# Scoring the sampled sequences' key pages four pairs at a time

## The chip, the cores and the metric

The kernel runs on one core of a Trainium2 chip. A core has TensorE (PE; its weight loads are listed as PEld), VectorE (DVE), ScalarE (ACT), GpSimd (POOL) and the queue engine SyncE (SP), and DMA engines that SP, ACT and POOL issue to. The metric is the device time of one execution in microseconds (us); the kernel before takes 1441.07 us in the median of three runs (1440.92 to 1441.21).

## The reference, cut to what matters

One inference step through two decoder layers: 256 prompt tokens and, in the same pass, 8 sampled sequences with 4 new tokens each. The second layer's mixer is sparse attention with three branches (compressed, selected blocks, window), 12 query heads on 3 key/value heads of width 64. For the selected-block branch each sampled sequence has 2048 past tokens in a paged cache: 16 pages of 128 tokens, whose numbers stand in `page_table`. The part that the change touches is the score of every sampled query against every past key of its own sequence:

```
k_b = cache_slc_kv[page_table[b]]            # sequence b: 16 pages x 128 tokens, 3 heads, 64 wide
s   = einsum('qhgd,nhd->qhgn', q_b, k_b)     # 4 tokens x 3 kv heads x 4 query heads x 2048 keys
s   = s * SCALE - slope * distance           # later: mask to the chosen blocks, softmax, values
```

## The kernel before, in words

The eight PSUM banks are handed back and forth by `banks`: `fill` (TensorE waits for a free bank), `filled`, `take` (a reader waits for a full bank), `give`, `wait_given`.

The stretch in question is a loop of TensorE over `n` = 0 to 13 (lines 879 to 892), about 895 to 1012 us into the span. It does two unrelated things side by side:

- Prompt attention in 12 units. In turn `n` TensorE scores unit `n+1` (`unit_scores`, L836 and L837), transposes the probabilities of unit `n-1` (`unit_turn`, L845) and multiplies unit `n-2` with its values (`unit_pv`, L860 and L862, and L856 in every second unit). Between these, VectorE adds the distance term and finds maxima (L1657 to L1662), ScalarE takes exponentials (L1246), VectorE normalises (L1669 to L1676), and ScalarE copies the transposes out.
- Key-page scores of the sampled sequences. Two sequences share the 128 partitions (an even one in the lower 64, an odd one in the upper 64), so there are four pairs `b`. A pair's stationary operand is 128 x 32 (`QBD[:, b, h, :]`). One scoring step (`page_scores`, L876) multiplies it with 512 keys, four pages, of head `h`: one matmul, 128 x 32 by 128 x 512, into 32 partitions of bank 7. ScalarE copies these to `S_SLC` (`scores_out`, recorded at the copy helper's line L1203) before the next step may fill bank 7. There are 4 pairs x 4 chunks of 4 pages x 3 heads = 48 steps, four in each turn from `n` = 2 to 13: after `unit_scores`, after `unit_turn`, and two after `unit_pv`.

The keys lie in the arena, in two halves of 16 pages' width each. Half `s` holds all 16 pages of one pair. SP loads the even sequences and POOL the odd ones (`load_key_pages`, L353 to L359), in rounds of four DMAs: a load of four page numbers into registers (L341), then for each page register work and one 96 KB DMA (L359). Pairs 0 and 1 are loaded before the loop starts; pair 2 is loaded once step 11 (the last of pair 0) has left its half, pair 3 after step 23. After step 35, SP loads the window keys into the lower half (`in_wink`, L1922) and after step 47 the window values into the upper half (`in_winv`, L1924).

After the loop TensorE turns the new values (L899), scores new tokens (L905, which waits for VectorE's copies of the queries, L1692, and these wait for the last `unit_pv`), compressed keys (L911) and window keys (L920, four pairs in the four column groups of the array). L920 releases the first value pages (L366), which SP and POOL load in the same kind of rounds into the arena, while the softmaxes run; the loads of the last sequences wait for the transposed probabilities (L973), and the last products with values (L952) wait for these pages.

Of the kernel before, what the change touches and what calls it, by code (L numbers as in the profile page):

```python
# [17 lines left out]
SP, POOL = mybir.EngineType.SP, mybir.EngineType.Pool  # L18

P = 128  # L20
# [3 lines left out]
B = 8  # L24
# [11 lines left out]
H = 3  # L36
G = 4
PAGE = 128
NPG = 16
PG_STEP = 4  # L40
# [3 lines left out]
WIN = 512  # L44
# [122 lines left out]
def trunk_kernel(nc, x_in, mem_in, cst1_in, cst2_in, slcd_in, prm_in, bmat_in, cmat_in, w8_in, wglu_in, wfi_in, wfo_in,  # L167
# [3 lines left out]
    with ctx:  # L171
# [12 lines left out]
        AR = sb("arena", 12288)  # L184
# [8 lines left out]
        PT = sb("pages", P, I32, 1)  # L193
# [83 lines left out]
        QBD = U[:, 8288:8672].rearrange("p (b h r) -> p b h r", b=4, h=H)  # L277
# [8 lines left out]
        S_SLC = U[:, 0:3 * 2080].rearrange("p (h n) -> p h n", h=H)  # L286
# [8 lines left out]
        KP = [AR[:, 6144 * s:6144 * s + 6144].rearrange("p (g h n) -> p g h n", g=NPG, h=H) for s in range(2)]  # L295
# [5 lines left out]
        BK = [ctx.enter_context(nc.psum_tensor(f"bank{b}", [P, 512], F32)) for b in range(8)]  # L301
        banks = Banks([sem(f"bank{b}_full") for b in range(8)], [sem(f"bank{b}_free") for b in range(8)])
# [22 lines left out]
        kpage_loaded = [[sem(f"key_pages{s}_{c}_loaded") for c in range(2)] for s in range(2)]  # L325
# [5 lines left out]
        qbd_done, q_done = sem("sample_query_blocks"), sem("sample_queries")  # L331
# [3 lines left out]
        ss_max, ss_exp, ss_prob = sem("sample_slc_max"), sem("sample_slc_exp"), sem("sample_slc_prob")  # L335

        def page_numbers(eng, which, b, i, pool_in):

            at = PT[0:1, bass.ds(i * PG_STEP + b * NPG, PG_STEP)]  # L340
            return nc.values_load_multi_w_load_instructions(at, engines=[which], min_val=0, max_val=pool_in.shape[0] - 1)[1]  # L341

        def page(pool_in, r):
            return pool_in[bass.ds(r, 1), :, :].rearrange("a p n -> p (a n)")

        def wait_memory_attention(eng, l, n):

            if n == 0:
                banks.take(eng, ("ms", l, 4))
            elif n == 1:  # L350
                banks.wait_given(eng, ("mo", l, 2))

        def load_key_pages(eng, which, b, s):  # L353

            with eng.Fori(0, NPG // PG_STEP) as i:
                for u, r in enumerate(page_numbers(eng, which, b, i, slck_in)):
                    lo = 64 * (b % 2)
                    dst = AR[lo:lo + 64, bass.ds(i * (384 * PG_STEP) + (6144 * s + 384 * u), 384)]
                    eng.dma_start(dst, page(slck_in, r)).then_inc(kpage_loaded[s][b % 2], 16)  # L359

        def load_value_pages(eng, which, b):
            s = VSLOT[b]
# [32 lines left out]
        n = 0  # L395
# [21 lines left out]
        def _(pe):  # L417
# [448 lines left out]

            def page_scores(step):

                b, c, h = step // 12, step // 3 % 4, step % 3
                if step % 12 == 0:  # L870
                    if b == 0:
                        pe.wait_ge(qbd_done, 1)
                    for parity in range(2):
                        pe.wait_ge(kpage_loaded[b % 2][parity], 256 * (b // 2 + 1))
                banks.fill(pe, ("sk", step), 7)
                ins = nc.tensor.matmul(BK[7][32 * b:32 * b + 32, :].rearrange("p (g n) -> p g n", n=P), QBD[:, b, h, :],  # L876
                                       KP[b % 2][:, 4 * c:4 * c + 4, h, :], start=True, stop=True)
# [160 lines left out]
        def _(act):  # L1038
# [193 lines left out]
                banks.give(C(PTC[0:NCP, 2 * n:2 * n + 2, :].rearrange("p g q -> p (g q)"), BK[5 + n % 2][0:NCP, :]), ("pct", n))  # L1232

            def scores_out(step):
                b, c, h = step // 12, step // 3 % 4, step % 3
                banks.take(act, ("sk", step))
                banks.give(C(S_SLC[32 * b:32 * b + 32, h, WIN * c:WIN * c + WIN], BK[7][32 * b:32 * b + 32, :]), ("sk", step))

            for n in range(14):
                if n < 12:  # L1240
                    act.wait_ge(u_max, n + 1)
                    for gg in range(2):
                        for t in range(2):
                            s = SU[n % 2][:, gg, P * t:P * t + P * (t + 1)]
                            j = 2 * t + gg
                            ins = A(s, s, ACT.Exp, bias=NM[n % 2][:, j:j + 1], accum_out=RS[n % 2][:, j:j + 1])  # L1246
                    ins.then_inc(u_exp, 1)
                if n >= 2:
                    scores_out(4 * (n - 2))
# [5 lines left out]
                if n >= 2:  # L1255
                    scores_out(4 * (n - 2) + 1)
# [4 lines left out]
                for j in range(2 if n >= 2 else 0):  # L1261
                    scores_out(4 * (n - 2) + 2 + j)
# [41 lines left out]
        def _(pool):  # L1304
# [71 lines left out]
            banks.take(pool, ("hc", 1, 1), B // 2 - 1)  # L1376
            query_blocks(1, 15)
            pool.wait_ge(memkv_stored, 32)
            for p in range(4):
                wait_memory_attention(pool, 1, p)  # L1380
                if p >= 2:
                    banks.take(pool, ("sk", 12 * p - 13))
                load_key_pages(pool, POOL, 2 * p + 1, p % 2)
# [6 lines left out]
        def _(dve):  # L1390
# [368 lines left out]
            banks.wait_given(dve, ("sk", 47))  # L1759
# [48 lines left out]
        def _(sp):  # L1808
# [106 lines left out]
            for p in range(4):  # L1915
                wait_memory_attention(sp, 1, p)
                if p >= 2:
# [5 lines left out]
            banks.take(sp, ("sk", 47))  # L1923
# [151 lines left out]
```

## Time and profile before

| | |
|---|---|
| timed runs | 1441.21, 1440.92, 1441.07 us |
| span of the profiled execution | 1438.6 us; the page gives no other time of it, so about 2.5 us of a run lie outside the span |
| PE busy | 1301.7 us (90% of the span) |
| DVE, ACT, POOL busy | 300.5, 247.6, 184.5 us |
| L876, key-page scores | 96 matmul instructions, 51.6 us busy, 11.5 us of PE idle time just before them |

Times in the rows below are microseconds from the start of the span. "Granted clock" is TensorE's clock as a share of full speed, 2.4 GHz; 0.50 means 1.2 GHz. A row of PE's timeline gives the start of a group of matmuls and the time to its modelled end; since matmuls overlap, the distance between the starts of two neighbouring rows is the better measure of what a piece costs.

### The profile page before, as it was taken

How to read it: one execution, taken by the hardware profiler on the slowest of the kernel's cores; microseconds unless marked ns; L12 is line 12 of the kernel's file. 1: busy time of each engine (PE TensorE's matmuls, PEld its weight loads, DVE VectorE, ACT ScalarE, POOL GpSimd, SP SyncE). 2: the span in 40 equal slices, each digit the busy share in tenths (PEclk: the TensorE clock that was granted, in tenths of full speed). 3: DMA queues.
4: the chain of work that ended last, by engine and by line, in shares of the span. 5: the costliest groups of instructions: out<-in, count | busy, mean ns of one | idle time of the engine just before them, and what ended most of it. 6: DMA issues, size and time to landing. Idle time of an engine off the chain costs nothing. (4 is left out here: it accounts for less than half of the span.)

```text
span 1438.6 us, 17417 instructions
## 1 busy us (share of the span) xinstructions
PE 1301.7 (90%) x6217; PEld 955.9 (66%) x6217; DVE 300.5 (21%) x670; ACT 247.6 (17%) x555; POOL 184.5 (13%) x254
## 2 busy tenths in 40 slices
PE   7969999999697999999989987898656889999996
PEld 6837666666675777777767866332445667777774
DVE  4112333432304000000040013432730130000002
ACT  3040011010112111100021112555310111010000
POOL 1002432534300000000000004031351000000000
PEclk9857999999598999999999956899877989999998
DMA  7605224330057343364333415043562314333332
GB/s 304 247 1 175 89 87 131 110 109 0 1 207 294 117 146 123 139 262 140 131 117 117 147 52 171 7 131 133 188 180 73 117 59 145 121 142 127 121 121 73
DMA packets 57937, 185.37 MB, mean 129 GB/s; under 512 B 8385, under 2 KB 39362, under 8 KB 47298
## 3 DMA queue, kind: packets, MB, share of 16 engines
q1 hardware_dynamic: 51314, 165.84, 34.0%
q0 software_dynamic: 6144, 12.59, 3.1%
q10 hardware_dynamic: 432, 6.29, 1.1%
q8 instruction: 32, 0.52, 0.2%
q14 instruction: 15, 0.12, 0.0%
HBM read 180.91 MB, written 10.02 MB: 133 GB/s over the span
## 5 line engine op out<-in xcount | busy, mean ns | idle before, releaser
L641 PE MATMUL bank<-normed,slabs 128*128 128x288 f32 x1408 | 347.2, 410 | 7.3 <-DVE normed L1406 7.3
L641 PEld LDWEIGHTS bank<-normed,slabs 128*128 128x128 f32 x1408 | 270.7, 192 | 83.8 <-issue 8.2
L670 PE MATMUL bank<-hidden,slabs 128*128 128x288 f32 x704 | 173.2, 406 | 1.9 <-DVE hidden L1444 1.9
L608 PE MATMUL bank<-arena,phase 128*128 128x384 f32 x512 | 170.7, 492 | 0.0
L670 PEld LDWEIGHTS bank<-hidden,slabs 128*128 128x128 f32 x704 | 133.6, 190 | 39.5 <-DVE hidden L1444 2.7
L608 PEld LDWEIGHTS bank<-arena,phase 128*128 128x128 f32 x512 | 96.9, 192 | 65.2 <-issue 1.5
L453 PE MATMUL bank<-normed,slabs 128*128 128x288 f32 x400 | 99.1, 411 | 3.7 <-DVE normed L1406 3.7
L453 PEld LDWEIGHTS bank<-normed,slabs 128*128 128x128 f32 x400 | 76.9, 193 | 25.5 <-issue 4.1
L1444 DVE TENSOR_TENSOR hidden<-projected,bank 128x288 f32 (+1 forms) x44 | 20.0, 454 | 322.6 <-PE bank L641 322.6
L581 PEld LDWEIGHTS bank<-projected,hidden 128*128 128x128 f32 x480 | 64.9, 220 | 6.3 <-DVE mixed L1536 2.9
L581 PE MATMUL bank<-projected,hidden 128*128 (+1 forms) x480 | 65.9, 302 | 2.7 <-DVE mixed L1536 2.7
L453 PE MATMUL bank<-mixed,slabs 128*128 128x288 f32 x256 | 66.5, 416 | 1.3 <-DVE mixed L1796 1.3
L1318 POOL COPY arena<-projected 64x32 f32<-64x32 f32 x8 | 1.6, 206 | 481.5 <-ACT projected L1064 481.2
L432 PE MATMUL bank<-normed,cst 128*128 128x288 f32 x128 | 45.9, 487 | 19.3 <-ACT normed L1044 11.5
L1399 DVE TENSOR_SCALAR rstd<-bank 128x288 f32<-128x288 f32 x8 | 3.7, 458 | 282.5 <-PE bank L432 282.5
L1110 ACT ACTIVATE normed<-bank 128x288 f32<-128x288 f32 x32 | 13.1, 410 | 285.1 <-PE bank L670 175.9
L876 PE MATMUL bank<-arena,phase 128*32 128x512 f32 x96 | 51.6, 620 | 11.5 <-ACT phase L1203 11.5
L453 PEld LDWEIGHTS bank<-mixed,slabs 128*128 128x128 f32 x256 | 49.9, 196 | 15.4 <-issue 1.4
L1119 ACT ACTIVATE projected<-bank 128x288 f32<-128x288 f32 x44 | 18.0, 410 | 202.1 <-PE bank L641 202.0
L359 POOL DMA_DIRECT2D arena<-in_slck x64 | 33.9, 530 | 124.2 <-issue 118.9
L432 PEld LDWEIGHTS bank<-normed,cst 128*128 128x128 f32 x128 | 28.7, 230 | 31.2 <-issue 20.2
L1338 POOL TENSOR_TENSOR phase_small<-normed,phase 128x512 f32<-128x512 f32 (+1 forms) x15 | 17.1, 1139 | 220.9 <-DVE normed L1555 220.9
(277 smaller groups left out, 1246.2 us busy)
## 6 DMA issues: line engine op xcount, KB each, us to landing
slabs<-in_wfi SPq DMA_DIRECT2D x44, 1024.0 KB, 4.7
slabs<-in_w SPq DMA_DIRECT2D x25, 1024.0 KB, 5.0
arena<-in_cmp SPq DMA_DIRECT2D x128, 192.0 KB, 2.7
slabs<-in_wfo SPq DMA_DIRECT2D x32, 704.0 KB, 4.0
arena<-in_slck SPq DMA_DIRECT2D x64, 96.0 KB, 2.9
arena<-in_slck POOLq DMA_DIRECT2D x64, 96.0 KB, 2.7
out_win_old<-in_winold SPq DMA_DIRECT2D x1, 6096.0 KB, 24.4
arena<-in_slcv POOLq DMA_DIRECT2D x48, 96.0 KB, 2.7
```

Of the source, the lines that this page charges most:

```text
L359: eng.dma_start(dst, page(slck_in, r)).then_inc(kpage_loaded[s][b % 2], 16)
L432: ins = nc.tensor.matmul(BK[7][:, 0:T], ones, Hn[:, m, :], start=(m == 0), stop=(m == 7))
L453: ins = nc.tensor.matmul(BK[b][:, 0:T], wt[:, k, c * P:c * P + P], rhs[:, k, :], start=(k == 0), stop=(k == kc - 1))
L581: ins = nc.tensor.matmul(BK[r][:, cc * width:cc * width + width], BT[r][:, c, :], tok(c // 4), start=True, stop=True)
L608: ins = nc.tensor.matmul(out.rearrange("p h (g s) -> p h g s", s=8), W1S[:, c, a, j, :], PG[u][:, :, c * 8 + j, :, :].rearrange("p g h s - ...
L641: ins = nc.tensor.matmul(BK[2 * (u % SLOTS) + c][:, 0:T], wt[:, k, c * P:c * P + P], Hn[:, k, :], start=(k == 0), stop=(k == KC - 1))
L670: ins = nc.tensor.matmul(BK[b][:, 0:T], wt[:, k, :], HD[:, 11 * kh + k, :], start=(kh + k == 0), stop=(kh * 11 + k == 21))
L876: ins = nc.tensor.matmul(BK[7][32 * b:32 * b + 32, :].rearrange("p (g n) -> p g n", n=P), QBD[:, b, h, :], KP[b % 2][:, 4 * c:4 * c + 4, h ...
L1110: A(Hn[:, m, :], BK[b][:, 0:T], ACT.Square).then_inc(sq_done, 1)
L1119: ins = A(Z[:, 8 + u % SLOTS, :], BK[2 * (u % SLOTS)][:, 0:T], ACT.Silu)
L1338: ch.tick(tt(hr, re, cos, ALU.mult))
L1444: banks.give(tt(dst, Z[:, 8 + u % SLOTS, :], BK[2 * (u % SLOTS) + 1][:, 0:T], ALU.mult), up)
```

## The change

The arena's halves no longer hold one pair each. Half `c % 2` now holds four pages, chunk `c`, of all eight sequences; so a scoring step `(c, h)` can be done for all four pairs at once. It issues four matmuls, one for each pair, to four different groups of 32 columns, which write the four quarters of bank 7, and ScalarE copies the whole bank, 128 x 512, in one operation. There are 12 steps instead of 48, one in each turn `n` from 2 to 13. The number of matmuls stays at 48, the DMAs and bytes stay the same, and the releases are renamed: chunk 2 is loaded after step 2, chunk 3 after step 5, the window keys after step 8, the window values after step 11.

```diff
-        KP = [AR[...].rearrange("p (g h n) -> p g h n", g=NPG, h=H) for s in range(2)]
+        KP = [AR[...].rearrange("p (b g h n) -> p b g h n", b=B // 2, g=PG_STEP, h=H) for s in range(2)]
...
-        def load_key_pages(eng, which, b, s):
-            with eng.Fori(0, NPG // PG_STEP) as i:
-                for u, r in enumerate(page_numbers(eng, which, b, i, slck_in)):
-                    lo = 64 * (b % 2)
-                    dst = AR[lo:lo + 64, bass.ds(i * (384 * PG_STEP) + (6144 * s + 384 * u), 384)]
-                    eng.dma_start(dst, page(slck_in, r)).then_inc(kpage_loaded[s][b % 2], 16)
+        def load_key_pages(eng, which, par, c):
+            s = c % 2
+            with eng.Fori(0, B // 2) as i:
+                at = PT[0:1, bass.ds(i * (2 * NPG) + (par * NPG + PG_STEP * c), PG_STEP)]
+                for u, r in enumerate(numbers_at(which, at, slck_in)):
+                    dst = AR[64 * par:64 * par + 64, bass.ds(i * (384 * PG_STEP) + (6144 * s + 384 * u), 384)]
+                    eng.dma_start(dst, page(slck_in, r)).then_inc(kpage_loaded[s][par], 16)
...
             def page_scores(step):
-                b, c, h = step // 12, step // 3 % 4, step % 3
-                if step % 12 == 0:
-                    if b == 0:
-                        pe.wait_ge(qbd_done, 1)
+                c, h = step // 3, step % 3
+                if step == 0:
+                    pe.wait_ge(qbd_done, 1)
+                if h == 0:
                     for parity in range(2):
-                        pe.wait_ge(kpage_loaded[b % 2][parity], 256 * (b // 2 + 1))
+                        pe.wait_ge(kpage_loaded[c % 2][parity], 256 * (c // 2 + 1))
                 banks.fill(pe, ("sk", step), 7)
-                ins = nc.tensor.matmul(BK[7][32 * b:32 * b + 32, :]..., QBD[:, b, h, :],
-                                       KP[b % 2][:, 4 * c:4 * c + 4, h, :], start=True, stop=True)
+                for b in range(B // 2):
+                    ins = nc.tensor.matmul(BK[7][32 * b:32 * b + 32, :]..., QBD[:, b, h, :],
+                                           KP[c % 2][:, b, :, h, :], start=True, stop=True)
                 banks.filled(ins, ("sk", step))
...
             for n in range(14):
-                more = iter(range(4 * (n - 2), 4 * (n - 1)) if n >= 2 else ())
                 if n < 11:
                     unit_scores(n + 1)
                 if n >= 2:
-                    page_scores(next(more))
+                    page_scores(n - 2)
                 if 1 <= n < 13:
                     unit_turn(n - 1)
                 if n >= 2:
-                    page_scores(next(more))
                     unit_pv(n - 2)
-                for step in more:
-                    page_scores(step)
...
-                banks.give(C(S_SLC[32 * b:32 * b + 32, h, WIN * c:WIN * c + WIN], BK[7][32 * b:32 * b + 32, :]), ("sk", step))
+                banks.give(C(S_SLC[:, h, WIN * c:WIN * c + WIN], BK[7][:, :]), ("sk", step))
...                                              # SP, and likewise POOL with parity 1
-            for p in range(4):
-                wait_memory_attention(sp, 1, p)
-                if p >= 2:
-                    banks.take(sp, ("sk", 12 * p - 13))
-                load_key_pages(sp, SP, 2 * p, p % 2)
-            banks.take(sp, ("sk", 35))
+            for c in range(NPG // PG_STEP):
+                wait_memory_attention(sp, 1, c)
+                if c >= 2:
+                    banks.take(sp, ("sk", 3 * c - 4))
+                load_key_pages(sp, SP, 0, c)
+            banks.take(sp, ("sk", 8))
```

On TensorE, one turn of the loop (here `n` = 3) before: the scoring steps are the rows of L876, `unit_turn` is L845, `unit_pv` is L860 and L862.

```order
L876 MATMUL bank<-arena,phase 32x512 [waits bank7_free]
L845 MATMUL bank<-cst,hidden 128x128 [waits bank4_free,unit_prob]
L845 MATMUL bank<-cst,hidden 128x128 x2
L845 MATMUL bank<-cst,hidden 128x128 [waits bank5_free]
L845 MATMUL bank<-cst,hidden 128x128 x2
L876 MATMUL bank<-arena,phase 32x512 [waits bank7_free]
L860 MATMUL bank<-normed 64x256 [waits bank4_free]
L862 MATMUL bank<-normed 64x128
L860 MATMUL bank<-normed 64x256 [waits bank5_free]
L862 MATMUL bank<-normed 64x128
L876 MATMUL bank<-arena,phase 32x512 [waits bank7_free] x2
```

The same turn after the change, where the lines stand two or three further down (the scoring matmul is L879):

```order
L879 MATMUL bank<-arena,phase 32x512 [waits bank7_free]
L879 MATMUL bank<-arena,phase 32x512 x3
L847 MATMUL bank<-cst,hidden 128x128 [waits bank4_free,unit_prob]
L847 MATMUL bank<-cst,hidden 128x128 x2
L847 MATMUL bank<-cst,hidden 128x128 [waits bank5_free]
L847 MATMUL bank<-cst,hidden 128x128 x2
L862 MATMUL bank<-normed 64x256 [waits bank4_free]
L864 MATMUL bank<-normed 64x128
L862 MATMUL bank<-normed 64x256 [waits bank5_free]
L864 MATMUL bank<-normed 64x128
```

Four single matmuls, each with its own wait for bank 7, have become one group of four with one wait, and nothing of the scoring is left between `unit_turn` and `unit_pv` or behind it.

On ScalarE, the same turn before, from the exponentials of the unit to the last of the four copies out of bank 7:

```order
L1246 ACTIVATE hidden,stats<-hidden,stats 128x128 [waits unit_max]
L1246 ACTIVATE hidden,stats<-hidden,stats 128x256
L1246 ACTIVATE hidden,stats<-hidden,stats 128x128
L1246 ACTIVATE hidden,stats<-hidden,stats 128x256
L1203 ACTIVATE phase<-bank 32x512 [waits bank7_full]
L1203 ACTIVATE normed<-bank 128x384 [waits bank4_full]
L1203 ACTIVATE normed<-bank 128x384 [waits bank5_full]
L1203 ACTIVATE phase<-bank 32x512 [waits bank7_full] x3
```

And after:

```order
L1245 ACTIVATE hidden,stats<-hidden,stats 128x128 [waits unit_max]
L1245 ACTIVATE hidden,stats<-hidden,stats 128x256
L1245 ACTIVATE hidden,stats<-hidden,stats 128x128
L1245 ACTIVATE hidden,stats<-hidden,stats 128x256
L1202 ACTIVATE phase<-bank 128x512 [waits bank7_full]
L1202 ACTIVATE normed<-bank 128x384 [waits bank4_full]
L1202 ACTIVATE normed<-bank 128x384 [waits bank5_full]
```

Three of the four copies are gone and the one that is left takes 128 partitions. The programs of SP and POOL have the same instructions in the same order as before, with the waits renamed.

## Rows read from the trace of the kernel before

**Rows 1.** Page, part 5: form and count; busy, mean ns; idle before, releaser.

```profile
L876 PE MATMUL bank<-arena,phase 128*32 128x512 f32 x96 | 51.6, 620 | 11.5 <-ACT phase L1203 11.5
```

**Rows 2.** PE timeline, turns 3 and 4: start, us, line, form, count, idle before.

```profile
916.27 0.49 PE L836 MATMUL bank<-projected 64*128 64x128 f32 x2
...
917.78 1.04 PE L876 MATMUL bank<-arena,phase 128*32 128x512 f32 x2
918.75 0.88 PE L845 MATMUL bank<-cst,hidden 128*128 128x128 f32 x6
919.56 1.04 PE L876 MATMUL bank<-arena,phase 128*32 128x512 f32 x2
920.53 0.65 PE L860 MATMUL bank<-normed 128*64 128x256 f32 x2
...
921.98 1.05 PE L876 MATMUL bank<-arena,phase 128*32 128x512 f32 x2
923.70 1.05 PE L876 MATMUL bank<-arena,phase 128*32 128x512 f32 x2 [0.68 <-ACT phase L1203]
924.68 0.48 PE L836 MATMUL bank<-projected 64*128 64x128 f32 x2
...
934.08 0.48 PE L836 MATMUL bank<-hidden,projected 64*128 64x128 f32 x2
```

**Rows 3.** PE timeline, window-key scores in four column groups.

```profile
1015.02 2.76 PE L920 MATMUL bank<-arena,phase 128*32 128x512 f32 x24
```

**Rows 4.** ACT groups by form, 900 to 1013 us: count; busy, mean ns; idle.

```profile
L1203 ACT ACTIVATE phase<-bank 32x512 f32<-32x512 f32 x48 | 28.2, 587 | 45.9 <-PE bank L876 45.4
...
L1203 ACT ACTIVATE mixed<-bank 128x512 f32<-128x512 f32 x3 | 1.8, 597 | 2.6 <-PE bank L862 2.6
```

**Rows 5.** DVE timeline of one unit, first and last operation.

```profile
919.72 1.02 DVE L1657 SCALAR_TENSOR_TENSOR hidden<-phase_small,bank 128x384 f32<-128x384 f32 x2 [6.42 <-PE bank L845]
...
922.30 1.01 DVE L1676 TENSOR_SCALAR hidden<-hidden,cmp_hidden 128x128 f32<-128x128 f32 x4
```

**Rows 6.** PE timeline, scoring steps 1 and 2 of turn 2.

```profile
909.55 1.65 PE L876 MATMUL bank<-arena,phase 128*32 128x512 f32 x2
911.13 1.07 PE L856 MATMUL bank<-hidden,s_small 15*64 15x256 f32 x4
...
913.58 1.04 PE L876 MATMUL bank<-arena,phase 128*32 128x512 f32 x2
```

**Rows 7.** Issues of L359 on SP, pair 2: ns min/median/max, first and last start.

```profile
L359 SPq DMA_DIRECT2D arena<-in_slck x1: 502/502/502, 935.9 to 935.9; - x1
...
L359 SPq DMA_DIRECT2D arena<-in_slck x4: 491/491/531, 949.6 to 951.8; - x4
```

**Rows 8.** Windows: us, busy PE, PEld, DVE, ACT, POOL; PEclk, DMA share, GB/s.

```profile
953.50:954.00 0.50, 0.50 (x2) 0.03 (x2) 0.00 (x0) 0.50 (x5) 0.00 (x0) 1.00 0.44 157
954.00:954.50 0.50, 0.50 (x3) 0.13 (x2) 0.00 (x0) 0.48 (x3) 0.00 (x0) 1.00 0.00 0
```

**Rows 9.** Windows, TensorE's granted clock (PEclk, third number from the end).

```profile
905.00:906.00 1.00, 1.00 (x5) 0.58 (x3) 0.93 (x4) 0.17 (x1) 0.00 (x0) 0.50 0.00 0
...
1000.00:1012.20 12.20, 9.48 (x32) 2.81 (x31) 0.99 (x4) 3.63 (x7) 0.00 (x0) 1.00 0.01 1
...
1020.00:1021.00 1.00, 0.00 (x0) 0.00 (x0) 0.97 (x2) 0.08 (x1) 0.57 (x1) 0.51 0.98 418
...
1025.00:1026.00 1.00, 0.70 (x3) 0.73 (x4) 0.82 (x7) 0.00 (x0) 0.91 (x2) 0.50 0.64 158
...
1030.00:1031.00 1.00, 1.00 (x14) 0.72 (x10) 1.00 (x1) 0.00 (x0) 0.91 (x2) 0.87 0.82 239
```

**Rows 10.** DVE and PE timeline behind the loop: query copies, new-token scores.

```profile
1009.54 1.09 DVE L1692 COPY normed<-projected 64x96 f32<-64x96 f32 x4 [17.99 <-PE bank L862]
...
1012.89 1.52 PE L905 MATMUL bank<-projected,normed 64*128 64x32 f32 x12
```

**Rows 11.** DMA issues: form, count, KB each, median us to landing.

```profile
arena<-in_wink SPq DMA_DIRECT2D x4, 768.0 KB, 6.3
```

More of the change, by code:

```diff
@@ L294, in trunk_kernel @@
         WV = AR[:, 6144:12288].rearrange("p (b t n) -> p b t n", b=B, t=4)
-        KP = [AR[:, 6144 * s:6144 * s + 6144].rearrange("p (g h n) -> p g h n", g=NPG, h=H) for s in range(2)]
+        KP = [AR[:, 6144 * s:6144 * s + 6144].rearrange("p (b g h n) -> p b g h n", b=B // 2, g=PG_STEP, h=H) for s in range(2)]
         VAL = [AR[:, 3072 * s:3072 * s + 3072] for s in range(4)] + [KV[:, :]] + [U[:, 3072 * s:3072 * s + 3072] for s in range(2)]
@@ L335, in trunk_kernel, with numbers_at @@
         ss_max, ss_exp, ss_prob = sem("sample_slc_max"), sem("sample_slc_exp"), sem("sample_slc_prob")
+        def numbers_at(which, at, pool_in):
+            return nc.values_load_multi_w_load_instructions(at, engines=[which], min_val=0, max_val=pool_in.shape[0] - 1)[1]
         def page_numbers(eng, which, b, i, pool_in):
-            at = PT[0:1, bass.ds(i * PG_STEP + b * NPG, PG_STEP)]
-            return nc.values_load_multi_w_load_instructions(at, engines=[which], min_val=0, max_val=pool_in.shape[0] - 1)[1]
+            return numbers_at(which, PT[0:1, bass.ds(i * PG_STEP + b * NPG, PG_STEP)], pool_in)
         def page(pool_in, r):
@@ L867, in page_scores @@
             def page_scores(step):
-                b, c, h = step // 12, step // 3 % 4, step % 3
-                if step % 12 == 0:
-                    if b == 0:
-                        pe.wait_ge(qbd_done, 1)
+                c, h = step // 3, step % 3
+                if step == 0:
+                    pe.wait_ge(qbd_done, 1)
+                if h == 0:
                     for parity in range(2):
-                        pe.wait_ge(kpage_loaded[b % 2][parity], 256 * (b // 2 + 1))
+                        pe.wait_ge(kpage_loaded[c % 2][parity], 256 * (c // 2 + 1))
                 banks.fill(pe, ("sk", step), 7)
-                ins = nc.tensor.matmul(BK[7][32 * b:32 * b + 32, :].rearrange("p (g n) -> p g n", n=P), QBD[:, b, h, :],
-                                       KP[b % 2][:, 4 * c:4 * c + 4, h, :], start=True, stop=True)
+                for b in range(B // 2):
+                    ins = nc.tensor.matmul(BK[7][32 * b:32 * b + 32, :].rearrange("p (g n) -> p g n", n=P), QBD[:, b, h, :],
+                                           KP[c % 2][:, b, :, h, :], start=True, stop=True)
                 banks.filled(ins, ("sk", step))
@@ L1234, in scores_out @@
             def scores_out(step):
-                b, c, h = step // 12, step // 3 % 4, step % 3
+                c, h = step // 3, step % 3
                 banks.take(act, ("sk", step))
-                banks.give(C(S_SLC[32 * b:32 * b + 32, h, WIN * c:WIN * c + WIN], BK[7][32 * b:32 * b + 32, :]), ("sk", step))
+                banks.give(C(S_SLC[:, h, WIN * c:WIN * c + WIN], BK[7][:, :]), ("sk", step))
             for n in range(14):
@@ L1248, in _ @@
                 if n >= 2:
-                    scores_out(4 * (n - 2))
+                    scores_out(n - 2)
                 if 1 <= n < 13:
@@ L1254, in _ @@
                         banks.give(C(PTU[(n - 1) % 2][:, gg, :], BK[4 + gg][:, 0:3 * P]), key)
-                if n >= 2:
-                    scores_out(4 * (n - 2) + 1)
                 if n >= 2 and (n - 2) % 4 == 3:
@@ L1260, in _ @@
                     banks.give(C(M[:, 2 * h:2 * h + 2, 0:TP], BK[6][:, :].rearrange("p (c n) -> p c n", c=2)), ("po", h))
-                for j in range(2 if n >= 2 else 0):
-                    scores_out(4 * (n - 2) + 2 + j)
             for j3 in range(2):
@@ L1378, in _ @@
             pool.wait_ge(memkv_stored, 32)
-            for p in range(4):
-                wait_memory_attention(pool, 1, p)
-                if p >= 2:
-                    banks.take(pool, ("sk", 12 * p - 13))
-                load_key_pages(pool, POOL, 2 * p + 1, p % 2)
+            for c in range(NPG // PG_STEP):
+                wait_memory_attention(pool, 1, c)
+                if c >= 2:
+                    banks.take(pool, ("sk", 3 * c - 4))
+                load_key_pages(pool, POOL, 1, c)
             for b in range(1, B, 2):
@@ L1757, in _ @@
             ch.step(ts(MS, IMP, 0.5 * TAKEN, NEG, ALU.is_gt, ALU.mult))
-            banks.wait_given(dve, ("sk", 47))
+            banks.wait_given(dve, ("sk", 11))
             dve.wait_ge(slcd_loaded, 16)
@@ L1914, in _ @@
             sp.wait_ge(memkv_stored, 32)
-            for p in range(4):
-                wait_memory_attention(sp, 1, p)
-                if p >= 2:
-                    banks.take(sp, ("sk", 12 * p - 13))
-                load_key_pages(sp, SP, 2 * p, p % 2)
-            banks.take(sp, ("sk", 35))
+            for c in range(NPG // PG_STEP):
+                wait_memory_attention(sp, 1, c)
+                if c >= 2:
+                    banks.take(sp, ("sk", 3 * c - 4))
+                load_key_pages(sp, SP, 0, c)
+            banks.take(sp, ("sk", 8))
             for b in range(4):
                 sp.dma_start(AR[:, 1536 * b:1536 * b + 1536], wink_in[b]).then_inc(wink_loaded, 16)
-            banks.take(sp, ("sk", 47))
+            banks.take(sp, ("sk", 11))
             sp.dma_start(AR[:, 6144:12288], winv_in).then_inc(winv_loaded, 16)
```

## The prediction

> **What bounds the kernel now.** I read the chain of waits first. Between about 905 and 1012 us it runs almost only through TensorE: scoring step, transposes, products, and after some scoring steps ScalarE's copy. No other engine and no DMA is in it there. The costliest groups of the page say the same: the scoring has 51.6 us of busy time and 11.5 us of idle time before it, released by the copy [rows 1]. Then the PE timeline of one turn shows what a turn is made of [rows 2]. By the distances of starts: `unit_scores` 1.51 (916.27 to 917.78), scoring 0.97, `unit_turn` 0.81, scoring 0.97, `unit_pv` 1.45, scoring 1.72 (0.97 of work and a gap until ScalarE has emptied bank 7), scoring 0.98. The sum is 8.41 us for turn 3; turn 4 takes 9.40 (924.68 to 934.08), since every second `unit_pv` has one product more. TensorE is the bound of the loop and scoring is more than half of it.
>
> Behind the loop, L905 starts at 1012.89 [rows 10] and everything after it hangs on it in a chain of waits (softmaxes, then the loads of the value pages, then the last products). So I forecast by how much earlier L905 starts and let the rest move along.
>
> **The change part by part.**
>
> *Four matmuls side by side.* Whether a group of four costs one or four is the largest question. The trace has the same shape with the same column groups: L920, 3 heads x 4 pairs x 2 passes = 24 instructions, takes 2.76 us including the end of the last [rows 3]. One after the other at the 0.97 of a two-pass step, 12 matmuls would take 11.6 us. A group of four there costs about 0.9 us, no more than one matmul. I take 0.98 for a step; the bounds are 0.92 (2.76 / 3) and 3.88 (4 x 0.97).
>
> The Trainium skill, page "TensorE: Matmul & The Clock Gate", section "Part 3: Packing small matmuls — row/col tiling", gives a measured gain of 2.38 for three column tiles, not 3. Carried over to four (an estimate from that page) a step would cost about 1.2 us and the loop 3 us more than I say. L920's row speaks for the full gain, and I go by the row.
>
> *Three steps less in each turn.* A turn loses 0.97 + 1.72 + 0.98 = 3.67 us: an odd turn becomes 8.41 - 3.67 = 4.74, an even one 9.40 - 3.67 = 5.73 [rows 2].
>
> *ScalarE.* Copying 128 x 512 takes 597 ns, 32 x 512 took 587 [rows 4]: 12 copies for 48, nothing added. The copy of a step is wanted a whole turn later, so no wait for bank 7 is left.
>
> *VectorE* now comes close. From the end of a `unit_turn` to the probabilities that let the next begin it needs 919.72 to 923.31, 3.59 us [rows 5]; with the 0.81 of the transposes and two hops of about 0.1 that is 4.6 us, under 4.74. It hides in the odd turns by only 0.1 us; were it worse by 0.3, the loop would lose 1 to 2 us.
>
> *Key pages.* The bytes are unchanged, the releases sit at the same turns (4 and 7), but the turns are shorter, and this cover is what goes. Before, step 11 ends at 934.08 [rows 2], SP's first issue starts at 935.9 and its fourth round at 949.6 [rows 7], so a round takes (949.6 - 935.9) / 3 = 4.6 us; the DMAs fall silent after 953.9 [rows 8]. So 19.9 us from release to landing, set by SP's rounds of register work and issue rather than by bytes.
>
> Now the calendar. Step 0 stays. Turn 2 loses 911.13 - 909.55 = 1.58 and 916.27 - 913.58 = 2.69 [rows 2, 6], so turn 3 starts at 912.0 and turn 4 at 916.74; step 2 ends at 916.74 + 1.51 + 0.97 = 919.2.
> Chunk 2 lands at 919.2 + 19.9 = 939.1. Step 6 wants it after the rest of turn 4 (3.25), turns 5, 6, 7 (4.74 + 5.73 + 4.74) and a `unit_scores` (1.51): 19.97 us, at 939.2. No wait, but nothing to spare either.
> Chunk 3 is released at step 5, when SP is still issuing chunk 2. Its four rounds queue behind: 4 x 4.6 = 18.4 us more, landing at 957.5. Step 9 wants it after the rest of turn 8 (4.22), turns 9 and 10 (4.74 + 5.73), with no `unit_scores` in turn 11: at 953.9. TensorE waits 3.6 us for it. This is a new wait, on SP's queue; behind it stand the last three turns and all that follows. POOL's rounds are shorter and it lands earlier.
>
> From step 9 at 957.5 remain three steps (3 x 0.98), two `unit_turn` (2 x 0.81) and three `unit_pv` (1.45 + 2.45 + 1.45): 9.9 us, to 967.4.
>
> *The clock.* After L920, TensorE is idle from 1017.8, and by 1020 its granted clock has gone from 1.00 to 0.50 (2.4 to 1.2 GHz); it returns at about 1030, when TensorE has been at work again since about 1025.3 [rows 3, 9]. The fall came 2.2 us into the idle time, and the wait at step 9 is longer, so I expect a fall there and, from the 4.7 us of work before the return, about 6 us of work at the half clock, which costs 3 us (bounds 0 and 5): 970.4.
>
> *Behind the loop.* The query copies (1.09 us) wait for the last `unit_pv`. Before, two scoring steps stood behind that and hid them; L905 started 3.4 us after the copies did [rows 10]. Now L905 waits for them, 1.3 us with the hops: L905 at 971.7.
>
> *Window keys and values.* SP issues the window keys when its last round ends, at about 957.5. They land 6.3 us (median of four) after issue [rows 11], by some 968, while L920 comes 2 us after L905. The values follow step 11 as before. Both hidden; 4 us is the margin.
>
> Sum: L905 moves from 1012.89 to 971.7, 41 us earlier. Against the profiled span: 1438.6 - 41 = 1397.6, and with the 2.5 us by which the median of the runs, 1441.07, is above the span: 1400.
>
> **The rivals.**
>
> A. *No new wait and no fall of the clock.* The rounds are a little quicker or the turns a little slower than I have them. Then L905 comes at 953.9 + 9.9 + 1.3 = 965.1, 48 us earlier: 1393. With the wait but without the fall it is 1397. For it: the wait is a difference of 3.6 us between two long sums. Against it: SP's rounds are the same instructions.
>
> B. *The clock falls inside the loop, in stretches.* What is left in a turn is much work with half the rows (`unit_scores`, 64) or 15 rows. At 905 to 906 such work kept PE busy for the whole microsecond at a granted clock of 0.50 [rows 9]. Two or three such stretches of 7 us cost 3.5 each: 1407 to 1415. Against it: at the loop's end PE was busy only 9.48 of 12.2 us and kept 1.00 [rows 9].
>
> C. *Slower: the clock stays at half through the whole loop.* One mechanism, from turn 3 on: with the full-height scoring gone the loop never earns the full clock again. Turns 3 to 10 then take twice 4 x (4.74 + 5.73), 83.8 us, and the tail 19.8, so the key wait vanishes and L905 starts at 912.0 + 83.8 + 19.8 + 1.3 = 1016.9, 4 us later than before: 1445. It decides from the point where more than about nine tenths of the loop run at 0.50. Against it: transposes and scoring, 128 rows high, are still 1.8 us of every turn, and `unit_pv` is too.
>
> D. *The four matmuls run one after the other.* Then the scoring work stays; what goes are the waits for the copies, 11.5 us [rows 1], with a little of the query copies lost: about 1430. Rows 3 speak against it as plainly as a trace can.
>
> **How the numbers follow.** Forecast as worked out, 1396 to 1405 around 1400: 0.58. A: 0.13. B: 0.18. D, or a step that costs well over one matmul: 0.06. C, or some other cover that breaks: 0.05. The range 1392 to 1416 takes in A, B and the bounds of the clock and of the key wait, and leaves out D and C. A measurement of this kernel can tell 0.2%, 3 us, from no change. Only C can be slower: 0.04 by over 0.2%; within 0.2%, a half-hearted C or D: 0.02; faster 0.94.
>
> **What would show it right or wrong.** Right: 12 groups of eight scoring instructions at about 1 us each; turns of 4.7 and 5.7 us alternating; a wait of 2 to 5 us before step 9 released by a DMA into the arena, and none or a short one before step 6; SP's rounds at 4.6 us without a gap between chunk 2 and 3; the granted clock at 0.50 for some microseconds after that wait and 1.00 in turns 4 to 10; L905 about 1.3 us behind the last product; from L905 to the end the same length as before within 2 us. Wrong: scoring groups of 3 to 4 us (D); a clock of 0.50 in turns 4 to 10 (B, C); turns of over 5.3 us with TensorE waiting for VectorE's probabilities; L920 waiting for the window keys.

## The result and the profile after

The changed kernel takes 1397.95 us, the median of four runs (1395.28 to 1410.09), beside 1441.14 for the kernel before (four runs, 1440.92 to 1445.86): ratio 0.9707, 95% interval 0.9658 to 0.9756. The forecast was 1400. The profiled run took 1399.01 us, its span is 1397.3 us. Single runs of the changed kernel lie 15 us apart here, and 18 us over all 17 of this study (1395.28 to 1413.76), so small differences are read below from lengths inside the profiles.

The scoring in the changed kernel, first from one line of code (ns min/median/max, first and last start), then from the groups of instructions by form, as [rows 1] shows it (count; busy, mean ns; idle before, releaser):

```profile
L879 PE MATMUL bank<-arena,phase x96: 592/617/1061, 902.8 to 967.6; 128*32 128x512 f32 x96
```
```profile
L879 PE MATMUL bank<-arena,phase 128*32 128x512 f32 x96 | 14.5, 681 | 3.7 <-DMA arena<-in_slck 3.7
```

The 96 instructions are still there, and one of them is as long as before: the median is 617 ns in both kernels (the mean is higher than in [rows 1], since two of the 12 steps ran at half the clock). But four lie side by side, so together they keep TensorE busy for 14.5 us instead of 51.6. The 11.5 us of waiting for ScalarE's copy are gone, and two waits for key pages, 3.7 us, stand in their place. The PE timeline of one turn, of the two steps that wait, and of the loop's end:

```profile
920.09 1.06 PE L879 MATMUL bank<-arena,phase 128*32 128x512 f32 x8
921.08 0.88 PE L847 MATMUL bank<-cst,hidden 128*128 128x128 f32 x6
921.89 1.07 PE L858 MATMUL bank<-hidden,s_small 15*64 15x256 f32 x4
...
924.33 0.49 PE L838 MATMUL bank<-hidden,projected 64*128 64x128 f32 x2
...
925.84 1.07 PE L879 MATMUL bank<-arena,phase 128*32 128x512 f32 x8
...
941.48 1.06 PE L879 MATMUL bank<-arena,phase 128*32 128x512 f32 x8 [0.32 <-DMA arena<-in_slck]
...
959.63 1.07 PE L879 MATMUL bank<-arena,phase 128*32 128x512 f32 x8 [3.34 <-DMA arena<-in_slck]
...
967.12 1.06 PE L879 MATMUL bank<-arena,phase 128*32 128x512 f32 x8
...
969.57 0.83 PE L898 MATMUL bank<-cst,projected 128*32 128x128 f32 x6
970.81 1.52 PE L904 MATMUL bank<-projected,normed 64*128 64x32 f32 x12 [0.42 <-DVE normed L1687]
```

From the scoring to the transposes behind it is 0.99 us for eight instructions, where [rows 2] had 0.97 for two. An even turn is 925.84 - 920.09 = 5.75 us (9.40 before). L904 is the L905 of [rows 10]: 970.81 for 1012.89. The chain of waits (start, length, what) shows where the key wait comes from:

```profile
936.68 0.53 SPq L361
...
941.25 0.49 SPq L361
...
945.83 0.53 SPq L361
...
950.44 0.52 SPq L361
...
955.04 0.53 SPq L361
...
957.18 2.41 DMA arena<-in_slck
959.63 1.07 PE bank L879 x8
```

Between 922.9 and 957.2 the chain is SP's sequencer, not TensorE. 936.68 starts the last round of chunk 2; the four rounds of chunk 3 follow, 4.6 us apart as in [rows 7] and without a gap; the last issue lands 2.4 us later and releases step 9.

The granted clock (last but two in a row) around the loop's start, with PE's busy time before it:

```profile
902.00:903.00 1.00, 1.00 (x7) 0.50 0.00 0
910.00:911.00 1.00, 1.00 (x5) 0.50 0.00 0
916.00:917.00 1.00, 1.00 (x6) 0.50 0.00 0
917.00:918.00 1.00, 1.00 (x6) 0.84 0.00 0
918.00:919.00 1.00, 1.00 (x8) 1.00 0.00 0
959.00:960.00 1.00, 0.37 (x4) 1.00 0.92 143
```

The same view of the kernel before, where step 0 began at 906.23:

```profile
909.00:910.00 1.00, 1.00 (x4) 0.50 0.00 0
910.00:911.00 1.00, 1.00 (x2) 0.60 0.00 0
911.00:912.00 1.00, 1.00 (x5) 1.00 0.00 0
```

Half speed lasts until 917.3, 14.5 us after step 0 began at 902.82; before, it ended at 910.8, 4.6 us after step 0. After the wait for step 9 the clock stays at 1.00 in this run.

To compare profiles I cut the span at four places: the first `unit_scores`, step 2, step 9, and the new tokens' scores (L904 here, L905 before). "Half speed" is the stretch from the clock's fall near the loop's start to its return, from slices of 1 us. All in us, from all profiles of this study:

| kernel | loop starts | to step 2 | step 2 to 9 | 9 to new tokens | loop | rest | half speed |
|---|---|---|---|---|---|---|---|
| before | 895.0 | | | | 117.9 | 425.7 | 13.7 |
| forecast | 895.0 | 23.2 | 39.3 | 14.2 | 76.7 | 425.7 | |
| changed | 891.6 | 28.5 | 39.5 | 11.2 | 79.3 | 426.5 | 23.9 |
| again | 891.2 | 28.5 | 40.2 | 12.8 | 81.5 | 425.0 | 23.9 |
| againb | 900.3 | 25.5 | 39.6 | 11.2 | 76.2 | 426.5 | 17.1 |
| againc | 890.9 | 28.5 | 40.0 | 13.5 | 82.1 | 424.5 | 23.9 |
| single | 894.2 | | | | 117.8 | 425.7 | 13.7 |
| wide | 900.4 | 29.0 | 53.2 | 18.8 | 100.9 | 425.7 | 13.7 |
| fourcopies | 897.0 | 28.6 | 39.5 | 11.5 | 79.6 | 426.3 | 23.9 |
| nochunk3 | 903.3 | 25.5 | 36.2 | 11.5 | 73.2 | 426.1 | 17.1 |
| shift | 899.7 | 13.4 | 39.8 | 20.0 | 73.1 | 426.0 | 10.2 |
| twice | 902.2 | 24.7 | 40.3 | 13.7 | 78.6 | 424.7 | 13.7 |
| spread | 891.5 | 13.4 | 46.2 | 11.5 | 71.1 | 425.1 | 10.2 |
| spreadb | 890.9 | 13.4 | 46.2 | 11.5 | 71.1 | 425.1 | 10.2 |

The rest is the same within 2 us in every row. So a profiled run's time is where its loop starts plus the length of its loop, and a constant. The first differs by 12 us between profiles, and the edits are hardly the reason: four profiles of one unaltered kernel have 890.9 to 900.3. The late ones had less clock ahead of the loop: the mean granted clock up to the loop's start is 0.91 where it starts by 891.6, and 0.89 where it starts at 903.3.

### The profile page after: what moved, and what is told of

It reads as the page before. It is cut to its first block and busy times, and to the rows that moved or that the text cites. A ratio compares the mean times of both kernels' runs of the same rounds, so it can differ in the third digit from the quotient of the medians.

```text
span 1397.3 us, 17381 instructions
## 1 busy us (share of the span) xinstructions
PE 1266.8 (91%) x6217; PEld 951.5 (68%) x6217; DVE 300.6 (22%) x670; ACT 226.0 (16%) x519; POOL 184.7 (13%) x254
## 5 line engine op out<-in xcount | busy, mean ns | idle before, releaser
L672 PEld LDWEIGHTS bank<-hidden,slabs 128*128 128x128 f32 x704 | 133.6, 190 | 39.5 <-DVE hidden L1439 2.7
L434 PE MATMUL bank<-normed,cst 128*128 128x288 f32 x128 | 45.8, 485 | 19.3 <-ACT normed L1043 11.5
L1333 POOL TENSOR_TENSOR phase_small<-normed,phase 128x512 f32<-128x512 f32 (+1 forms) x15 | 17.1, 1139 | 220.9 <-DVE normed L1550 220.9
```

Source lines behind the costliest of these rows:

```text
L434: ins = nc.tensor.matmul(BK[7][:, 0:T], ones, Hn[:, m, :], start=(m == 0), stop=(m == 7))
L672: ins = nc.tensor.matmul(BK[b][:, 0:T], wt[:, k, :], HD[:, 11 * kh + k, :], start=(kh + k == 0), stop=(kh * 11 + k == 21))
L1333: ch.tick(tt(hr, re, cos, ALU.mult))
```

## The experiments

**again, againb, againc: the changed kernel unaltered**, three times.

> The changed kernel once more, unaltered, for its spread and as the yardstick of this chip. Both theories: median 1398 us, single runs between 1395 and 1410. If TensorE's clock at the loop's start is what makes the spread, the profile shows the same turns (4.74 and 5.74 us) and the same wait of about 3 us before step 9, and only the time between step 0 and the return to the full clock (14.3 us in the first profile) differs; if the key loads make it, the wait differs.

> The changed kernel unaltered, for a third look at its loop. Theory: loop 79 to 82 us, full clock back 13 to 15 us after step 0's start, a wait of 3.2 to 4 us ahead of step 9 and under 0.6 us ahead of step 6. Rival (the late return of the clock is chance): it is back within 6 us of step 0's start in this run and the loop is under 77 us.

> The changed kernel unaltered, the partner of the run before. Theory: loop 76 to 82 us, step 2 to step 9 39.5 to 40.3 us whatever the clock does ahead of it, median 1397 to 1404 us. Rival: step 2 to step 9 follows the turns and not SyncE's rounds, and is under 39 or over 41 us.

Medians 1403.09 (six runs; ratio 0.9732, 0.9691 to 0.9773; I had expected 1398) and 1402.29 (six runs; ratio 0.9734, 0.9688 to 0.9781), and 1404.63 for the one run of againb. Step 2 to step 9 is 39.5 to 40.2 us in all four profiles, whatever the clock did ahead of it, as SP's rounds have it. The loop is 76.2 to 82.1 us, a little wider than expected on both sides. In again the clock returned 14.5 us after step 0, as in the first profile, so its return there does not make the difference between these two. In againb half speed ended 8.0 us after step 0, neither the 13 to 15 of the theory nor the 6 of the rival, and its loop of 76.2 us is the one that the rival had (under 77): how late the clock returns differs between runs. And in againc the fall that the prediction placed behind the wait is there, in again shorter, in the first profile and in againb not at all. The fall does not follow from the length of the wait alone: none comes with waits of 3.34 and 3.39 us (the first profile, againb), one with 3.84 and 3.87 (again, againc). The windows of againc:

```profile
957.00:958.00 1.00, 0.00 (x0) 0.79 0.58 158
958.00:959.00 1.00, 0.00 (x0) 0.50 1.14 220
963.00:964.00 1.00, 1.00 (x4) 0.50 1.05 436
964.00:965.00 1.00, 1.00 (x7) 0.80 0.98 412
```

It falls while TensorE waits for chunk 3 and returns some 7 us later; step 9 to the new tokens is 13.5 there against 11.2 without a fall: 2.3 us.

**single: the new layout of the keys, the grouping undone.**

```
-                for b in range(B // 2):
-                    ins = nc.tensor.matmul(BK[7][32 * b:32 * b + 32, :]..., QBD[:, b, h, :], KP[c % 2][:, b, :, h, :], ...)
+                ins = nc.tensor.matmul(BK[7][32 * b:32 * b + 32, :]..., QBD[:, b, h, :], KP[c % 2][:, b, :, h, :], ...)
...                     # 48 steps, four in a turn and a copy for each, as before
```

> The new layout of the key pages is kept (four pages of all eight sequences in a half), the grouping is undone: 48 steps of one matmul with a copy of 32 x 512 each, four in a turn, at the places they had before; releases after steps 11, 23, 35 and 47. Theory (the gain is the grouping, the layout alone is worth nothing): turns of 8.4 and 9.4 us again, no key waits, 1439 to 1443 us. Rival (the loads of four pages of all sequences at a time bring something by themselves): 1400 to 1435 us.

1441.88 us (ten runs), ratio 0.9994, 0.9965 to 1.0023. Its page has the group of [rows 1] again:

```profile
L878 PE MATMUL bank<-arena,phase 128*32 128x512 f32 x96 | 51.5, 619 | 11.5 <-ACT phase L1205 11.5
```

Loading the pages in another order is worth nothing by itself; it is what the grouping needs.

**wide: four matmuls in a group, but none beside another.** Each takes 128 columns and writes all partitions of the bank; the scores are then not the four pairs'.

```
-                    ins = nc.tensor.matmul(BK[7][32 * b:32 * b + 32, :]..., QBD[:, b, h, :],
+                    ins = nc.tensor.matmul(BK[7][:, :]..., U[:, 8288 + 64 * b:8416 + 64 * b],
```

> A step still issues four matmuls of 512 columns one behind the other and one copy, but each takes 128 columns of queries and writes all 128 partitions of the bank, so that no two can stand side by side in column groups; the scores of a step are then not the four pairs' (only the time is looked at). It tells the column groups from the rest of the change (one copy per step, no wait for the bank between pairs). Theory: the side-by-side work is the gain. A step takes 3.9 us instead of 0.99, turns 7.65 and 8.65 us; step 2 to step 9 takes 35.9 + 7 x 2.9 = 56 us and both waits for keys vanish; loop 100 to 107 us against 79.3, 81.5 and 76.2 in the three profiles of the changed kernel and 117.9 before; time 1419 to 1428 us. Rival: what went was the waiting for bank 7 and for the copies, and four matmuls in one group cost about one whatever their columns: a step of 1 to 1.5 us, loop 76 to 84 us, time 1395 to 1406 us.

1427.73 us (six runs), ratio 0.9887, 0.9845 to 0.9928; loop 100.9 us. The theory holds. PE timeline of one odd turn:

```profile
937.64 3.70 PE L879 MATMUL bank<-arena,phase 128*128 128x512 f32 x8
941.18 0.82 PE L847 MATMUL bank<-cst,hidden 128*128 128x128 f32 x6
...
944.88 3.70 PE L879 MATMUL bank<-arena,phase 128*128 128x512 f32 x8
```

A step takes 3.54 us instead of 0.99 (I had expected 3.9), a turn 7.24 us instead of 4.75. It is not the width of a product that costs: one of the four takes 0.89 us, no more than the 0.97 of one with 32 columns. So of the 38 us that the changed loop is shorter than the one before, 17 (117.9 - 100.9) come without column groups: 11.5 from the waits for copies [rows 1], some 4 because four matmuls behind one another take 3.54 and not 4 x 0.97, 12 times (the last 1 to 2 us I can't assign); side by side brings the other 21 (100.9 less the mean of 79.8), net of the key waits and the slower clock that appear with it. The Trainium skill's page "TensorE: Matmul & The Clock Gate", section "Part 3: Packing small matmuls — row/col tiling", has a gain of 2.38 for three column tiles, from which I estimate 3.2 for four. Here four gain 3.54 / 0.99 = 3.6, so the measurement, and the row I went by [rows 3], is the better guide.

**fourcopies: the group as in the change, but four copies of 32 partitions.**

```
-                banks.give(C(S_SLC[:, h, WIN * c:WIN * c + WIN], BK[7][:, :]), ("sk", step))
+                for b in range(B // 2):
+                    ins = C(S_SLC[32 * b:32 * b + 32, h, WIN * c:WIN * c + WIN], BK[7][32 * b:32 * b + 32, :])
+                banks.give(ins, ("sk", step))
```

> The four groups of a step are still issued one behind the other and the layout is the changed one, but ScalarE copies each step's scores in four copies of 32x512 (587 ns each in the kernel before) instead of one of 128x512 (597 ns). Theory of the prediction: the copy hides beside TensorE's turn, so 1.76 us more of it per step costs little; ScalarE's own work of a turn becomes about 5.2 us against turns of 4.75 and 5.75, so at most 0.5 us in every second turn: loop 79.3 to 82.5 us, time 1398 to 1404 us. Rival: the copies of the transposes stand behind the four copies on ScalarE and TensorE's next products wait for them, so that most of the 1.76 us of each of the 12 steps shows: loop 92 to 101 us, time 1412 to 1420 us, with a wait for ScalarE ahead of the prompt's value products in every turn.

1402.18 us (four runs), ratio 0.9712, 0.9671 to 0.9753; loop 79.6 us. ScalarE's rows of a turn:

```profile
937.80 2.37 ACT L1202 ACTIVATE phase<-bank 32x512 f32<-32x512 f32 x4
940.20 0.87 ACT L1202 ACTIVATE normed<-bank 128x384 f32<-128x384 f32 x2
```

1.8 us more of copying per step hides, but for one wait of 0.26 us ahead of step 10. What the copies cost before was that TensorE stood waiting for one between two steps of a turn.

**nochunk3: the last four pages of each sequence are not loaded**; steps 9 to 11 score what lies in the buffer.

```
-                if h == 0:
+                if h == 0 and c < 3:
...
-            for c in range(NPG // PG_STEP):
+            for c in range(NPG // PG_STEP - 1):          # on SP and on POOL
```

> The keys of chunk 3 are not loaded (steps 9 to 11 score the keys of chunk 1 that lie there), so their scores are not the reference's; all else as in the changed kernel. Theory: the wait before step 9 (3.3 us) is SP's second set of rounds and goes altogether, nothing takes its place, and the loop's end, with all behind it, comes 3.3 us earlier: 1394 to 1395 us. Rival (something else was as late, such as VectorE's probabilities or the window keys): a new wait before step 9, before a transposition or before L919, and 1397 to 1399 us.

1401.11 us (four runs), ratio 0.9682, 0.9633 to 0.9732. Step 9 follows the products of the turn before without idle time, and step 2 to 9 takes 36.2 us instead of 39.5 to 40.2. The wait before step 6 stays at 0.36 us. So loading chunk 3 is the wait, 3.3 to 4 us. The run drops POOL's loads of that chunk together with SP's; that SP's are the later ones is read from the first profile, where POOL's last round starts at 952.81 and SP's at 955.04. The time of 1394 to 1395 us that I had expected did not come: the median lies among those of the changed kernel. The profiled run took 1404.29 us with a loop of 73.2, because that loop began at 903.3.

**shift: step n is scored in turn n instead of n + 2.**

```
-                if n >= 2:
-                    page_scores(n - 2)
+                if n < 12:
+                    page_scores(n)                        # scores_out on ScalarE likewise
```

> Every scoring step two turns earlier (step n in turn n, 0 to 11), nothing else. Theory (SP's rounds, started by step 2, set when step 9 can run, 38.5 us after step 2): the last key wait shrinks from 3.3 us to 0 to 1 us, because step 2 now comes before the slow first turns, and step 6 no longer waits; the two steps of turns 0 and 1 fall partly into TensorE's 1.8 us of idle time there: 1392 to 1395 us. Rival (the wait follows its release wherever it stands, seven turns apart as before): the wait stays 3 us and the time is 1397 to 1399 us.

1400.36 us (six runs), ratio 0.9709, 0.9666 to 0.9752, not the 1392 to 1395 expected. The loop is 73.1 us, 6 to 9 shorter than in the three profiles of the changed kernel that start early, and 3 shorter than in againb, which starts as late as this one. PE timeline, steps 8 and 9:

```profile
945.59 1.06 PE L879 MATMUL bank<-arena,phase 128*32 128x512 f32 x8
952.81 1.93 PE L879 MATMUL bank<-arena,phase 128*32 128x512 f32 x8 [1.40 <-DMA arena<-in_slck]
```

Step 2 to 9 remains 39.8 us, because SP's rounds begin at step 2 wherever that stands; the idle time before step 9 is only 1.40 because TensorE reaches it later by its own work (in turn 9 it still has a `unit_scores`, and in turn 2 it waits 0.96 us for VectorE's probabilities). The clock falls behind this short wait too, to 0.50 from 952.8 to 956.2. The larger part of the gain is at the start: half speed lasts 10.2 us, 7 to 14 less than in the changed kernel, and at half the rate that is 3 to 7 us.

**twice: the group of step 0 is issued two times.**

```
-                for b in range(B // 2):
+                for b in [0, 1, 2, 3] * (2 if step == 0 else 1):
```

> The group of step 0 is issued twice (eight matmuls where the changed kernel has four); nothing else differs. Loop length is counted from the first score product of unit 0 to the new tokens' scores; it was 79.3 and 81.5 us in two profiles of the changed kernel, with the full clock back 14.3 us after step 0's start. Theory: the full clock comes back late because the work of turns 2 and 3 is mostly products with 15 or 64 rows and only four of 128 rows where the kernel before had more; with a second group of 128 rows beside the first the clock is back at most 9 us after step 0's start, which takes some 6 us out of half speed and so about 3 us off the loop, against 1 to 1.9 us for the four products added: loop 77 to 79.5 us, time 1395 to 1402 us. Rival: when the clock returns has nothing to do with which products stand there; it is back 14 us or more after step 0, and the loop is longer by the added 1.9 us: 81 to 83.5 us, 1400 to 1406 us.

1399.89 us (five runs), ratio 0.97, 0.9661 to 0.9739; loop 78.6 us, inside the theory's range. Its windows at the loop's start:

```profile
913.00:914.00 1.00, 1.00 (x6) 0.50 0.00 0
916.00:917.00 1.00, 1.00 (x8) 0.50 0.00 0
917.00:918.00 1.00, 1.00 (x9) 0.57 0.00 0
918.00:919.00 1.00, 1.00 (x7) 1.00 0.00 0
```

The clock is back 4.4 us after step 0 began at 913.47, and half speed lasts 13.7 us, as in before, single and wide, which also spend more on products of 128 rows in turn 2 than one group does: in these four, all work from step 0 to the clock's return 4.3 to 4.6 us later has 128 rows, while with one group the products of 15 rows (L858) begin 3.3 us after step 0 and the clock is still at 0.50. The six profiles with one group there (changed, again, againb, againc, fourcopies, nochunk3) have 17.1 to 23.9. From step 0 to the clock's return PE is busy without a gap in both kinds; what differs is which products stand there. (The expectation's "only four of 128 rows" leaves out the transposes and the products with values, which have 128 rows too.) That four more matmuls shorten this is shown by one profile of this kernel. Chance has a part in the length too, but it does not explain the order. In before, wide, againb and nochunk3 the clock falls 2.2 us behind the loop's start; among these half speed lasts 13.7 us with the additional products and 17.1 with one group. In the other six it falls 1.9 to 2.0 us behind it; there the two lengths are 13.7 (single, twice) and 23.9. The loop as a whole gains nothing to speak of over 76.2 to 82.1, since the wait before step 9 is there (3.82 us) and the clock falls behind it.

**spread, spreadb: steps 0 to 2 in turns 0 to 2, 3 to 8 in turns 4 to 9, 9 to 11 in turns 11 to 13.**

```
+        STEP_AT = [0, 1, 2, 4, 5, 6, 7, 8, 9, 11, 12, 13]
...
-                if n >= 2:
-                    page_scores(n - 2)
+                if n in STEP_AT:
+                    page_scores(STEP_AT.index(n))         # scores_out likewise
```

> Steps 0 to 2 are scored in turns 0 to 2, steps 3 to 8 in turns 4 to 9, steps 9 to 11 in turns 11 to 13; turns 3 and 10 score nothing. Step 2 then stands nine turns (some 44 us) ahead of step 9, where SyncE's two sets of rounds need 2 times 18.4 us and a landing of 2.4 us, 39 us. Theory: the wait ahead of step 9 (3.3 us in the changed kernel, 1.4 us with step n in turn n) is gone, and the fall of the clock behind it with it: loop 70 to 72.5 us against 79.3 and 81.5, a median some 7 us under the changed kernel's on the same chip. Rival 1: the turns without scoring leave TensorE thin work only, the clock falls there and costs 2 to 4 us: loop 73 to 76 us. Rival 2: the keys come later than counted, because SyncE's rounds are slowed by other transfers: a wait of over 1 us ahead of step 9 stays.

> The kernel with steps 0 to 2 in turns 0 to 2, 3 to 8 in turns 4 to 9 and 9 to 11 in turns 11 to 13 again, beside the changed kernel on one chip. Theory: its loop is again 70 to 73 us, without a wait for keys at step 9, and its median is 4 to 9 us under that of the changed kernel beside it (loop 76 to 82). Rival: the gain in the loop is given back behind it, in waits for pages or in another phase of the clock: the two medians are within 2 us.

1395.53 us (six runs; ratio 0.9675, 0.9638 to 0.9711) and 1398.86 us (six runs; ratio 0.9697, 0.9659 to 0.9734). The loops are 71.1 us in both, as expected. PE timeline of spread:

```profile
943.24 0.87 PE L848 MATMUL bank<-cst,hidden 128*128 128x128 f32 x6
...
947.84 0.87 PE L848 MATMUL bank<-cst,hidden 128*128 128x128 f32 x6 [0.79 <-DVE hidden L1672]
...
950.78 0.38 PE L865 MATMUL bank<-normed 128*64 128x128 f32 x2
951.09 1.07 PE L880 MATMUL bank<-arena,phase 128*32 128x512 f32 x8
```

Step 9 waits for no page, and the clock is 1.00 from 904 to the new tokens. Where a turn has no scoring, TensorE waits for VectorE's probabilities instead: transposes to transposes is 4.60 us.

The median on one chip is 3.4 us under againc's, just short of the 4 to 9 expected; the means there differ by 6.3 us. Over all runs of this study the 12 of this version average 1396.3 and the 17 of the changed kernel 1403.0 us: 6.7 us less, 95% interval 2.3 to 11.0 from the scatter of the runs. By the loops it should be 8.6 (79.8, the mean of four, less 71.1). So it is faster than the kernel before on both chips. Over the changed kernel the lead is plain in the loops, but in the times it is clear only with the runs of several chips put together: on the one chip that has six runs of each, the interval of the 6.3 us is -1.8 to 14.3.

## Why the prediction was right

The new tokens' scores start 42.1 us earlier in the first profile (forecast 41), of which 3.4 us are an earlier loop start and 38.7 the shorter loop; over four profiles the loop is 38.1 shorter. So the time came out 2 us from the forecast with help from where that profile's loop began, which was luck; the mechanism is right, two sizes are not.

- *A group costs one matmul.* Forecast 0.98, measured 0.99; wide shows that this is the columns' doing. Rival D falls: its 1430 is about what wide, which is D built, takes.
- *Turns.* 4.75 and 5.75, forecast 4.74 and 5.73.
- *ScalarE adds nothing.* Right, and fourcopies shows how much room there was.
- *VectorE just under the turn.* The forecast 4.6 us is the 4.60 of spread's turn without scoring; in the changed kernel TensorE is the later one.
- *Key pages.* Step 6 waits 0.28 to 0.45 us where none was forecast with nothing to spare; step 9 waits 3.34 to 3.87 for a forecast 3.6, and nochunk3 with the chain shows that SP's rounds of chunk 3 are the reason. Rival A, no wait, did not come.
- *The clock, the step that was mis-sized.* "After the wait" I charged 3 us; measured 0, 1.6, 0 and 2.3, a mean of 1.0. I had taken a longer wait as enough for a fall; waits of 3.3 to 3.4 us had none, and shift's 1.40 had one. And I let turns 2 and 3 keep the clock they had before. They did not: with scoring steps gone from turn 2 (before, step 1 at 909.55 [rows 6] stood where the clock returned, at 910.8) the full clock came back 3 to 10 us later, and step 2 stands 28.5 us behind the loop's start instead of 23.2 in three profiles of four, 25.5 in the other. That is rival B's mechanism, in one stretch at the loop's start where I had looked for it in turns 4 to 10; these ran at 1.00. It costs 2 to 5 us.
- *Behind the loop.* L904 waits for the query copies: it starts 1.24 us behind L898, forecast 1.3 behind the last product. The rest is 424.5 to 426.5 us for 425.7 before. Rival C, half speed throughout, fell with the clock's return. Outside the span lie 1.7 us and not the 2.5 that I added, as the profiled runs of all kernels after the change have it (1.6 to 1.7).

The errors nearly cancel: +5.3 (start), +0.2 (step 2 to 9) and -3.0 (behind step 9) make the first profile's loop 79.3 for a forecast 76.7; -3.4 for its start and +0.8 for the rest bring the span to 1397.3, forecast 1397.6. In the range, rival B's upper end is too high by its own sum: three stretches of 3.5 us on 1400 are 1410.5 and not 1415. The result is far from both.

## What to carry to other kernels

Products with few columns of queries can be grouped so that four run in the time of one (0.99 us for 0.97 here); lay the loaded data out so that all four operands are there together, and some of the gain (here 11.5 us of 38) is the waits for a shared bank that go. When a loop gets that much shorter, recompute the calendar of every queue that was hidden behind it, issue work included: here SP's rounds became the chain, and moving the step that releases a buffer earlier and the one that needs it later, without changing the work, took that wait away. Look too at what the removed work did for the clock.

## What the runs showed that I had not expected

- TensorE stayed at 0.50 for 23.9 us, though it was busy in all but 1.8 of them and without a gap in the last 18; products of 64 and 15 rows were about half of what it did. In the kernels with more products of 128 rows in turn 2 it was 13.7 us.
- The start of the loop varies by 12 us between profiles and the loop's own clock by 6.8 us of half speed between runs of one kernel, so that six runs leave a median uncertain by several us; the cut into start, loop and rest, of which the last is constant within 2 us, told kernels apart that the medians did not.
